# A tenth first product, low weights before low activations, and one load moved up in a one-core hybrid decoder layer

## What is computed

```python
h = rmsnorm(x, norm_pre) * (1.0 + scale) + shift
u_pool, z_pool, u_ssm, z_ssm, g_pool, g_ssm = split(h @ w_in)      # six parts of 1024 columns
y_pool = causal_pool_mixer(u_pool, pool_w, pool_scale) * silu(z_pool)
y_ssm = s5_mixer(u_ssm, ...) * silu(z_ssm)      # diagonal complex state space, gelu, sigmoid GLU
merged = sigmoid(g_pool) * (y_pool @ w_branch_pool) + sigmoid(g_ssm) * (y_ssm @ w_branch_ssm)
out = merged @ w_out
return x + gate * rmsnorm(out, norm_post)
```

## Time and profile before

| | us |
|---|---|
| median of 3 runs | 934.12 |
| lowest, highest | 933.94, 934.65 |
| profiled execution, its own time | 933.93 |
| span of its instructions | 932.1 |
| TensorE busy | 909.8 (98%) |
| VectorE busy | 726.2 (78%) |
| ScalarE busy | 389.0 (42%) |
| GpSimd busy | 45.3 (5%) |

### The profile page before, as it was taken

How to read it: one execution, slowest core, us unless ns; L and a number is a source line. 1 busy time by engine, 2 the same in 40 slices (tenths; PEclk the granted TensorE clock), 3 DMA queues, 4 the chain that set the end, 5 groups by cost and what they waited for, 6 DMA issues and landing times.

```text
span 932.1 us, 11810 instructions
## 1 busy us (share of the span) xinstructions
PE 909.8 (98%) x4312; PEld 763.3 (82%) x4312; DVE 726.2 (78%) x1057; ACT 389.0 (42%) x534; POOL 45.3 (5%) x82
## 2 busy tenths in 40 slices
PE   3999999999999999999999999999999999999996
PEld 3888888888888888888888888888888888887885
DVE  5988899887777888546789589948468786679977
ACT  5841353343444444344544353623144460136443
POOL 0019900000000000000000000000000000000000
PEclk9999999999999999999999999999999999999999
DMA  9843265545455364437799676476355268454233
GB/s 351 313 142 106 118 228 184 163 159 158 161 195 184 143 225 175 180 75 199 191 265 244 132 198 156 132 247 231 114 226 203 95 225 320 182 198 154 76 106 135
DMA packets 97449, 169.85 MB, mean 182 GB/s; under 512 B 38768, under 2 KB 55280, under 8 KB 97392
## 3 DMA queue, kind: packets, MB, share of 16 engines
q1 hardware_dynamic: 87600, 164.55, 54.1%
q10 hardware_dynamic: 9792, 4.56, 1.9%
HBM read 121.88 MB, written 47.19 MB: 181 GB/s over the span
## 4 chain that ended last, share of the span: by engine, by line
PE 96%; DVE 1%; ACT 1%; DMA 1%; issue 0%; ACTq 0%; DVEq 0%
PE ps L2537 41%; PE ps L2691 32%; PE psb L2691 13%; PE ps L2762 2%; PE psb L2742 2%; PE psb L2751 2%; PE psa L2730 2%; PE psa L2617 1%; PE psa L2537 1%; DMA par_are<-in_a_re 1%; PE psb L2617 0%; PE psb L2567 0%; ACT gt L1196 0%; DVE mod_out L1747 0%; PE psa L2567 0%
## 5 line engine op out<-in xcount | busy, mean ns | idle before, releaser
L2537 PE MATMUL ps<-bop,w_hi 128*128 128x512 f32 x864 | 232.2, 391 | 0.8 <-DVE bop L1789 0.8
L2537 PEld LDWEIGHTS ps<-bop,w_hi 128*128 128x128 f32 x864 | 161.2, 188 | 33.7 <-issue 0.9
L2537 PE MATMUL ps<-bop,w_lo 128*128 128x512 f32 x432 | 133.0, 389 | 0.0
L2537 PEld LDWEIGHTS ps<-bop,w_lo 128*128 128x128 f32 x432 | 81.1, 188 | 17.0
L2691 PE MATMUL ps<-bop,r_hi 128*128 128x512 f32 x272 | 83.7, 389 | 0.0
L1743 DVE TENSOR_TENSOR w_lo<-raw,w_hi 128x1024 fp32r<-128x1024 f32 x35 | 43.4, 1239 | 37.8 <-ACT w_hi L1182 37.5
L1182 ACT ACTIVATE w_hi<-raw 128x1024 fp32r<-128x1024 f32 x35 | 36.9, 1053 | 76.6 <-PE ps L2537 68.4
L2691 PEld LDWEIGHTS ps<-bop,r_hi 128*128 128x128 f32 x272 | 51.1, 188 | 10.6
L2691 PE MATMUL ps<-t_hi,r_hi 128*128 128x512 f32 x140 | 55.1, 393 | 0.0
L2691 PE MATMUL ps<-t_hi,r_lo 128*128 128x512 f32 x140 | 54.6, 390 | 0.0
L2691 PE MATMUL ps<-t_lo,r_hi 128*128 128x512 f32 x140 | 54.5, 389 | 0.0
(11 more groups left out here) (464 smaller groups left out, 1889.0 us busy)
## 6 DMA issues: line engine op xcount, KB each, us to landing
raw<-in_wstream SPq DMA_DIRECT2D x36, 512.0 KB, 5.4
pair_raw<-in_wstream SPq DMA_DIRECT2D x30, 512.0 KB, 4.2
ada<-in_w_ada SPq DMA_DIRECT2D x16, 512.0 KB, 11.3
x_tok<-in_x SPq DMA_DIRECT2D x8, 512.0 KB, 7.0
gs_d<-gt SPq DMA_DIRECT2D x8, 512.0 KB, 4.9
win_d<-win_new SPq DMA_DIRECT2D x8, 512.0 KB, 2.7
wout_d<-wout_new SPq DMA_DIRECT2D x8, 512.0 KB, 3.8
wout<-wout_d SPq DMA_DIRECT2D x8, 512.0 KB, 4.8
```

Of the source, the lines that this page charges most:

```text
L2537: last = mm(ps[slot(u)][:, f * HALF:f * HALF + HALF], a[:, k, :], b(k, f), start=k == order[0] and q == 0, stop=k == order[-1] and q == 2)
```

## The change

Four edits. The product of tile 7 of silu(z) goes from `FILL` of turn 0 to the end of `FIRST`, with its evacuation, its store and its weight loads; the jobs after it keep their banks, except `up` 0. To fit, the pairs swap banks and result buffers (`side`), and the semaphores for the banks change accordingly. In the three products that run step by step, the low weights times the high half of h come second and the high weights times the low half of h third, so that a step begins behind `h_hi_done` and waits for `h_done` only before its last two matmuls. And the load of `win` for turn 1 is issued ahead of the tables of turn 1.

```diff
-FIRST = [("gs", n) for n in range(KT)] + [("zs", 0)]
+FIRST = [("gs", n) for n in range(KT)] + [("zs", 0), ("zs", 7)]
-FILL = {0: [("zs", 7)], 4: [("zp", 6)], 7: [("zp", 7)]}
+FILL = {4: [("zp", 6)], 7: [("zp", 7)]}
 def side(j):
-    return (j + (j < NP)) % 2
+    return j % 2
...
             store_gs(6)
+            load_w(9)
             sp.wait_ge(coef_ready, 2)
...
-            sp.dma_start(zs_d[0], gt[0][:, :]).then_inc(zs_stored, 16)
+            sp.dma_start(zs_d[0], gt[0][:, :]).then_inc(zs_stored[0], 16)
+            sp.wait_ge(job_out[slot(("zs", 7))], evicted(("zs", 7)))
+            sp.dma_start(zs_d[7], gt[1][:, :]).then_inc(zs_stored[1], 16)
...
             load_u(1)
-            load_tables(1)
             for m in range(KT):
                 sp.wait_ge(x_done, m + 1)
                 if not last:
                     load_win(m + 1)
+                if m == 0:
+                    load_tables(1)
...
-                if m == 1:
-                    sp.wait_ge(job_out[slot(("zs", 7))], evicted(("zs", 7)))
-                    sp.dma_start(zs_d[7], zs_last).then_inc(zs_stored, 16)
...
             pair_high(0, P3)
+            act.wait_ge(gs_stored[1], 16 * 4)
+            evac(("zs", 7), gt[1][:, :], ACT.Silu)
             pair_high(0, P4)
...
             t_sums(3)
+            split_lo(9)
...
                 elif o >= 4:
-                    dve.wait_ge(mm_done, JOB[FIRST[-1 if o < 6 else -2]] + 1)
+                    dve.wait_ge(mm_done, JOB[FIRST[-2 if o < 6 else -1]] + 1)
...
-                pe.wait_ge(h_done, k + 1)
-                last = k_step(u, k, *h)
+                pe.wait_ge(h_hi_done, k + 1)
+                hi, lo = (wx_hi, wx_lo) if n == 2 else (w_hi[n % 2], w_lo[n % 2])
+                for q, (a, part) in enumerate(((hi, h[0]), (lo, h[0]), (hi, h[1]))):
+                    if q == 2:
+                        pe.wait_ge(h_done, k + 1)
+                    for f in range(2):
+                        last = mm(ps[slot(u)][:, f * HALF:f * HALF + HALF], a[:, k, :], part(k, f),
+                                  start=k == 0 and q == 0, stop=k == KT - 1 and q == 2)
...
             begin(turn0)
-            pe.wait_ge(c21_done, NP - 1)
+            pe.wait_ge(c11_done, NP)
             pe.wait_ge(c12_done, NP - 1)
```

More of the change, by code:

```diff
@@ L410, in build @@
         vta = ssm("vta", [P, GB, CH, SG])
-        zp_t = [t[:, :] for t in (gt[1], rt[1], gt[0], rt[0])]
+        zp_t = [t[:, :] for t in (gt[0], rt[0], gt[1], rt[1])]
         zp_t += [t[:, :, :].rearrange("p g c -> p (g c)") for t in (cos_pa, sin_pa)]
         zp_t += [vta[:, :, :, :].rearrange("p g t h -> p (g t h)"), pu[:, :, :].rearrange("p t c -> p (t c)")[:, 0:SEQ]]
-        zs_last = zp_t[6]
         pfix = ssm("pfix", [P, CH, 2])
@@ L532, in build @@
         gs_stored = two("gs_stored")
-        zs_stored = sem("zs_stored")
+        zs_stored = two("zs_stored")
         y_loaded = [sem(f"y_loaded{w}") for w in range(4)]
@@ L1058, in _ @@
             sp.wait_ge(in_lo_done, KT)
-            sp.wait_ge(zs_stored, 32)
+            for s in range(2):
+                sp.wait_ge(zs_stored[s], 16)
             sp.wait_ge(sq_ready, KT)
@@ L1298, in pair_high @@
                 elif o >= 4:
-                    act.wait_ge(mm_done, JOB[FIRST[-1 if o < 6 else -2]] + 1)
+                    act.wait_ge(mm_done, JOB[FIRST[-2 if o < 6 else -1]] + 1)
                 u = pair_weights(j)
@@ L1326, in copy_p1 @@
                     act.wait_ge(pair_stored[j % 2], 32 * (j // 2))
[L1327 to L1330, removed]
+                if j < 2:
+                    act.wait_ge(zs_stored[j], 16)
                 act.wait_ge(st_done, S_POS[j, P1] + 1)
@@ L1503, in _ @@
                 for u in FILL.get(m, ()):
[L1504 to L1507, removed]
+                    dst = zp_t[u[1]]
+                    if u == ("zp", 7):
                         act.wait_ge(pooled, KT)
@@ L2624, in half_product @@
                 if i == P1:
-                    if j == 0:
+                    if j == 1:
                         pe.wait_ge(job_out[0], SLOT[:len(FIRST)].count(0))
@@ L2653, in half_product @@
                     else:
-                        pe.wait_ge(job_out[j], SLOT[:len(FIRST)].count(j))
+                        pe.wait_ge(job_out[1 - j], SLOT[:len(FIRST)].count(1 - j))
                 elif i == P7:
@@ L2786, in _ @@
                 if m == 0:
-                    pe.wait_ge(c11_done, NP)
+                    pe.wait_ge(c21_done, NP)
                     pe.wait_ge(c12_done, NP)
```

## The result

| | before | changed |
|---|---|---|
| median, us (15 runs each) | 934.23 | 936.00 |
| lowest, highest | 933.70, 934.70 | 935.28, 937.15 |
| profiled execution, its own time | 933.93 | 936.34 |
| span of its instructions | 932.1 | 934.5 |

The changed kernel is slower: the ratio is 1.0021, with a 95% interval of 1.0013 to 1.0029. The median grew by 1.8 us and the profiled execution by 2.4. The executions also lie further apart than before, over 1.9 us instead of 1.0.

The account below looks back on a forecast made before the run. TensorE was taken to set the end between 26 and 924 us, each new wait paid in full. The terms -0.4 + 1.3 + 1.4 - 0.06 = +2.2 us gave a median of 936.3, range 934.4 to 938.0.

Parts of the forecast that it names:

- Low weights before low h: First products: first step starts without its wait, second tile's step at 28.98 instead of 29.37, so -0.4 us stays.
- Tile 7 as tenth product: End of the first products: its low weights are ready in time, 3.2 us of cover, so it costs 0.
- The load of `win` 1 ahead of the tables: SyncE's queue: lands by 436.1, costs nothing, and spares the old order's landing at 438.9 against `part_b(1)` at 436.1.
- First wait: Turn 0, `part_states(0)`: TensorE waits for `sq`, 1.3 us (1.1 to 1.5), having lost tile 7's cover.
- Second wait: `part_taps(1)`: the last taps land 16.0 us after `sq`, behind tables 2 in SyncE's queue; 1.4 us (0 to 2.4).
- rival (a): Only the wait for `sq` appears, taps landing as in the old turn 1: +0.8 us, median 934.9; chance 0.15.
- Turn 3: Small hiccup at `part_taps(3)` (2.01 instead of 1.95) goes, as turn 3 has more lead: -0.06 us.
- The sum: Whole kernel: +2.2 us on the profiled execution's 933.93, giving 936.2; 936.3 for the median, +0.23%.
- (b): Not slower: no wait at all if `sq` is complete by 439.5 or TensorE comes later; 933.7; chance 0.09.
- (d): First products: the reordering does nothing, the second tile holds the start; +0.4 on the sum, 936.7; no separate chance.
- Rival (c): A third wait: late SyncE queue also misses turn 2's or 3's loads; up to +5.0 us, 939.1; chance 0.09.

Follow-up runs that it names:

- e3_tables: Changed kernel with the four loads of tables 2 moved in SyncE's queue behind win 2, u 2 and taps 1: median 936.16 us, ratio 1.0022.
- e4_split: Changed kernel, in turn 0 VectorE's split for up 2 behind the scans and the pool's low half behind the outward rotation: 936.11 us, ratio 1.0024.
- e3_again: The kernel of e3_tables run again unchanged for a second profile: profiled execution 936.48 us.
- e3_third: The kernel of e3_tables run again unchanged for a third profile: profiled execution 936.27 us.
- e7_swap: Changed kernel with e4_split's VectorE order, and ScalarE's first swap ahead of the high half of up 2's weights: 935.59 us, ratio 1.0015.
- e5_all: Changed kernel with e7_swap's order in turn 0 and e3_tables' place of tables 2: 935.87 us, ratio 1.0017.
- e11_stores: e10_under with ScalarE's eight stores of y issued behind its second swap in turns 1 to 6: 933.26 us, ratio 0.9995 to the kernel before.
- e8_tables24: Changed kernel with tables 2 moved behind taps 1 and tables 4 behind taps 3 in SyncE's queue: 934.94 us, ratio 1.0010.
- e10_under: e8_tables24 plus e7_swap's order, with the split of low weights under ScalarE's swap in every turn: 935.35 us, ratio 1.0011.

## Why the prediction was right

**What bounds.** TensorE sets the end, and each new wait was paid in full: in the table's twelve rows within 0.35 us.

**Low weights before low h, -0.4.** The second tile's step starts at 28.95 instead of 29.37, with 0.30 of idle time left before it: -0.4, as said. The profile puts that idle time down to VectorE's split, which was over at 28.68; ScalarE's scaling, behind which I had put the step, ended later, at 27.64 + 1.20 = 28.84. I had not seen that the gain needs the other edit: alone it is lost again at the first pair.

**Tile 7 as tenth product, 0.** No wait at its head or among the pairs; the small gap before the first pair's P6 is gone.

**The load of `win` 1 ahead of the tables.** It lands in time. But the 2.8 us that the old order "would have cost here" were 1.6 at their place, and nothing in the time.

**First wait, 1.3.** Measured 1.21. `sq` is complete 1.16 us after TensorE gets to `part_states(0)` (451.13 - 449.97), predicted 1.17; what was mis-sized is the step from `sq` to TensorE's start, 0.05 instead of 0.14. One thing was left out of the working: the first swap stands behind the weights of `up` 2, which land just then (ScalarE was idle for them for 0.26 us). Here that cost nothing. The swap is over at 437.41 + 1.02 = 438.43, and VectorE is busy without a gap until it begins the rotation at 439.04; in e3_tables, where ScalarE didn't wait for these weights, the first wait is 1.20. Only where the split is gone from ahead of the rotation does the landing count (e4_split: VectorE idle for 1.11).

**Second wait, 1.4.** In sum 1.66, of which 0.12 stands at that place in e3_tables without any wait. I had put it all at `part_taps(1)`; half of it was u 2, at `part_b(2)`. The size was right because the distance behind it was: the taps landed 16.1 us after `sq` (the issue row at 459.05 ends at 464.16, its last issue takes 0.6 and landed 3.7 later, 467.27, less 451.13), predicted 16.0 from the earlier trace rows. That it fits this well is luck, for two errors of 1 us cancel: the last of the taps went out 12.4 us after `sq` instead of 11.3 (SyncE took 2.24 us to issue the two sine tables, in turn 3 before 1.24), and landed in 3.7 instead of 4.7. The rule that speaks for rival (a), some 2.0 us fixed plus bytes over 436 GB/s by the Trainium skill ("DMA: Bandwidth & Descriptors", section "Anatomy of one DMA — SWDGE (gpsimd) path"), would have the taps land in 2.0 us, as an estimate. The trace doesn't agree with it at this place: 3.7.

**Turn 3, -0.06.** Its hiccup is gone: 0.00.

**The sum.** +2.2 predicted on the profiled execution, +2.4 measured; 936.3 against a median of 936.0. In the trace the +2.4 are -0.59 at the start of `part_b(0)` (433.73 against 423.44 + 10.88) and +3.00 on the path. Rival (a) falls with the landing of 3.7, (b) with the wait for `sq`, (d) with the start at 28.95. Rival (c) needs a correction: its third wait does exist, though not in the changed kernel. In e3_again, e3_third, e7_swap and e5_all it stands in place of waits that were taken away (1.25 to 1.62 us); in e4_split, whose chain is longer, it stands beside them (0.62); in the first profile of e3_tables it hardly shows (0.08).

**What I had not understood** is that the waits are no list of costs. Beside TensorE runs one chain: `part_b(0)`, swap, rotation, scans, swap and `sq` of turn 0, the same of turns 1 and 2, with y's stores issued inside it, then tables 4, `win`, u 4 and taps 3. Before, tile 7's product gave TensorE 10.88 us more for the same stretch, and the chain kept up (79.55 us in which nothing was late), because TensorE set its pace: VectorE idled 4.34 us for `up` 1 ahead of the pooling of turn 1. In the changed kernel it goes from `sq` 0 into that pooling without a gap, and waits for TensorE again only at the second pool product in turn 2 (1.40 us, the row at 474.89). With the first waits shortened it hardly waits there either (0 in e3_again, e3_third, e7_swap and e5_all, 0.25 in e3_tables), so an earlier TensorE no longer brings `sq` of turn 2 forward. Without tile 7's product TensorE needs 68.67, the chain 70 to 72, and the difference is paid, at whichever of five places TensorE meets the chain first. My sum came out right because I had followed the chain to one late meeting point (taps 1), and the lag collected there covers the later ones. An account of single waits would have promised 1.6 us from e3_tables; it gave none in the median.

**What stays open.** Why executions of one kernel lie so far apart. The three profiles of e3_tables' kernel show one part of it: the landing of the last taps of turn 3, 3.2 us in one and 4.9 and 5.2 in the others, which TensorE pays for with the chain on its path. Why they land so differently isn't seen. The spreads by themselves prove little: that of the kernel before goes from 0.8 to 1.8 us in different rounds, and e11_stores spreads over 0.8 in those in which the kernel before does too. The medians of e8_tables24 and e10_under lie 0.3 and 1.2 us above their profiled executions, and no profile shows a long execution of them, so what was late in those wasn't seen.

## What to carry to other kernels

A product taken out of a stretch takes cover away from every chain beside it. Compare the two lengths over the whole stretch up to the last place at which they meet, not wait by wait: the cost is the difference, and repairing one wait can move it to the next meeting point. Shorten the chain itself, and look in it first for things that only stand there by order: weights' halves ahead of a swap, loads behind a semaphore they don't need, stores issued ahead of the copy on which the next step hangs. And take the time of a variant from its median: one profiled execution of e3_tables promised 1.5 us that ten others did not give.

## What was not expected of the hardware

Issuing transfers holds an engine, but only for what stands behind the issues: eight stores of 64 KB took ScalarE 4.43 and 5.61 us to issue, and its next copy waited for all of them (e10_under); placed behind the copies, the first three went out in 1.32 us from 460.22 on, beside the first copy of 1.06 us from 460.21 on (e11_stores). And the landing of an 8 KB load was no constant of its size: 2.0 us, 3.7 in the changed kernel, 4.7, and at one place of one kernel 3.2, 4.9 and 5.2 in three executions (e3_tables and its two repeats).
